# Turning key pages on VectorE in 32x32 blocks, with query rows and score rows laid out for it, in a hybrid decoder step

## The reference, cut to what matters

```python
h = rmsnorm(x, norm_g)
proj = jnp.einsum('bsd,de->bse', h, w_in)                  # 544 x 1024 by 1024 x 5632
q, k, v, g_a, u, v_s, g_b, m_a, m_b = jnp.split(proj, SPLIT_POINTS, axis=-1)
u = jax.nn.gelu(u)
v_s = layernorm(jax.nn.gelu(v_s), ln_g, ln_b)
...
# sample attention (moba_sample), for each of 8 samples, 16 cached pages of 128 keys x 8 heads x 64
k_full = cache_k[layer, page_table[:, :n_full * ppb]]
k_mean = jnp.mean(k_full.reshape(db, n_full, 256, N_HEADS, HEAD_DIM), axis=2)
gate = jnp.einsum('bthd,bnhd->bhtn', q, k_mean)            # 8 blocks of 256 keys
_, sel = lax.top_k(gate, 3)                                # three of them count
s_sel = jnp.einsum('bthd,bhtkd->bhtk', qf, k_sel) + bias
p = jax.nn.softmax(jnp.concatenate([s_sel, s_loc], axis=-1), axis=-1)
out = einsum(p_sel, v_sel) + einsum(p_loc, v_loc)          # per head and new row
...
y_a = attn * jax.nn.silu(g_a);  y_b = sgu * jax.nn.silu(g_b)
mixed = sigmoid(m_a) * (y_a @ w_pa) + sigmoid(m_b) * (y_b @ w_pb)
x = x + mixed @ w_o;  y = rmsnorm(x, final_norm_g)
```

## Time and profile before

| | |
|---|---|
| median of 3 runs | 582.92 us (582.87 to 583.2) |
| the profiled execution | 582.58 us |
| its span in the trace | 580.8 us |
| mean granted TensorE clock | 0.996 of full speed |
| busy: TensorE, VectorE, ScalarE, GpSimd | 98%, 54%, 36%, 4% of the span |
| the loop in the trace | 98.6 to 491 us |
| DMA over the span | 111.89 MB, mean 193 GB/s |

### The profile page before, as it was taken

One profiled execution on the slowest core, in us unless ns is written; L12 is line 12 of the kernel. 1 busy time (PEld: TensorE's weight loads), 2 busy tenths in 40 slices (PEclk: granted clock), 3 DMA queues, 4 the chain that ended last, 5 costly groups with the idle time before them and its releaser, 6 DMA issues.

```text
span 580.8 us, 14930 instructions
## 1 busy us (share of the span) xinstructions
PE 568.4 (98%) x6072; PEld 524.6 (90%) x6072; DVE 311.8 (54%) x733; ACT 210.4 (36%) x457; POOL 24.3 (4%) x39
## 2 busy tenths in 40 slices
PE   8999999999999999999999999999999999999994
PEld 6999999999999999999989998999999999998763
DVE  6622324344556465575757666785463354695514
ACT  5523222234333434444445442241252241234313
POOL 2101111000000000000000000010000000000002
PEclk9999999999999999999999999999999999999998
DMA  8447334765675756768577587875879856252003
GB/s 262 136 165 237 112 112 130 205 197 160 189 261 175 252 187 199 234 203 252 149 235 221 182 269 250 276 247 170 258 243 331 279 185 252 67 186 82 2 8 145
DMA packets 73421, 111.89 MB, mean 193 GB/s; under 512 B 5485, under 2 KB 35194, under 8 KB 73354
## 3 DMA queue, kind: packets, MB, share of 16 engines
q1 hardware_dynamic: 71978, 107.33, 57.7%
q0 software_dynamic: 1232, 3.36, 2.0%
q10 hardware_dynamic: 144, 0.26, 0.1%
HBM read 106.39 MB, written 4.53 MB: 191 GB/s over the span
## 4 chain that ended last, share of the span: by engine, by line
PE 93%; DVE 3%; ACT 1%; issue 1%; POOL 0%; POOLq 0%; DVEq 0%; ACTq 0%
PE BK L520 42%; PE BK L666 9%; PE BK L540 8%; PE BK L872 7%; PE BK L678 6%; PE BK L692 5%; PE BK L602 2%; PE BK L743 2%; PE BK L750 2%; PE BK L554 2%; PE BK L761 1%; PE BK L797 1%; PE BK L892 1%; PE BK L587 1%; PE BK L575 1%
## 5 line engine op out<-in xcount | busy, mean ns | idle before, releaser
L520 PE MATMUL BK<-XH,WH 128*128 128x272 f32 x672 | 212.2, 316 | 0.0
L520 PE MATMUL BK<-XH,WL 128*128 128x272 f32 x672 | 194.6, 290 | 0.0
L520 PE MATMUL BK<-XL,WH 128*128 128x272 f32 x672 | 193.5, 288 | 0.0
L520 PEld LDWEIGHTS BK<-XH,WH 128*128 128x128 f32 x672 | 127.0, 189 | 8.7 <-issue 8.0
L520 PEld LDWEIGHTS BK<-XL,WH 128*128 128x128 f32 x672 | 127.4, 190 | 0.0
L520 PEld LDWEIGHTS BK<-XH,WL 128*128 128x128 f32 x672 | 126.7, 188 | 0.0
L1165 DVE TENSOR_TENSOR WL<-WRAW,WH 128x1024 fp32r<-128x1024 f32 x51 | 62.2, 1220 | 37.9 <-ACT WH L921 37.6
L666 PE MATMUL BK<-CST,KRAW 128*128 128x128 f32 x512 | 77.2, 273 | 1.4 <-DVE ATS L1354 0.9
L666 PEld LDWEIGHTS BK<-CST,KRAW 128*128 128x128 f32 x512 | 60.5, 141 | 3.2 <-issue 3.1
L1263 DVE COPY KT<-BK 128x512 f32<-128x512 f32 x64 | 44.0, 687 | 35.3 <-PE BK L666 35.2
L921 ACT ACTIVATE WH<-WRAW 128x1024 fp32r<-128x1024 f32 x52 | 54.9, 1056 | 18.6 <-PE BK L540 18.6
(11 more groups left out here) (205 smaller groups left out, 796.6 us busy)
## 6 DMA issues: line engine op xcount, KB each, us to landing
KRAW<-in_cache_k SPq DMA_DIRECT2D x128, 256.0 KB, 3.5
VRAW<-in_cache_v SPq DMA_DIRECT2D x120, 256.0 KB, 3.9
WRAW<-in_w_in SPq DMA_DIRECT2D x21, 1024.0 KB, 5.5
WO<-in_w_o SPq DMA_DIRECT2D x4, 1024.0 KB, 7.9
XR<-in_x_prompt SPq DMA_DIRECT2D x4, 512.0 KB, 5.2
VEX<-in_cache_v SPq DMA_DIRECT2D x8, 256.0 KB, 5.1
WRAW<-in_w_pb SPq DMA_DIRECT2D x4, 512.0 KB, 6.3
WRAW<-in_w_pa SPq DMA_DIRECT2D x4, 512.0 KB, 5.8
```

The source lines that it names most:

```text
L520: last = mm(BK[h][:, 0:HALF], w[:, n % 2, k, :], x[:, k, cols], start=(i == 0 and w is WH and x is XA), stop=(i == KC - 1 and w is WL))
```

## The change

**Keys.** `turn_page` and both `page_out` are gone. VectorE turns each page with one operation, `dve.transpose`, from KRAW to KT. It turns every 32x32 block of the 128x512 page in its place: what was key 32g + m in partition, column 32f + d, stands afterwards in partition 32g + d, column 32f + m. The partitions so keep the key's quarter g, and only the lower five bits are swapped. `KR` goes from 5 to 4, the places of KT from 6 to 8.

**Scores.** A matmul sums over partitions, and these now mix four key quarters with 32 values of the head's width. So the queries are spread: QW holds, for each of 16 slices f of the width and each quarter, the 4 new rows of one sample at 8 columns of its own and zeros elsewhere. `page_scores` then sums over k (two halves of the head's width for two heads, each in its own columns) for each head pair c, with a moving operand that takes 32 columns from each of four pages. The rows of a score bank are now (head pair, key quarter, head of the pair, new row), its columns (page, key in the quarter). Sixteen matmuls before the loop and a copy bring the query rows (QR); GpSimd spreads those of one sample into QW (`query_rows`, four operations each). SCB is doubled (BK4 and BK2).

**Statistics.** All sums and masks follow the new rows: 128 rows of local scores, constant matrices OVER and TOTAL in place of SUM, 40 columns of R. `choose` writes the masked scores as a copy of all 512 columns (SC), and ScalarE takes one exponential over it. The local probabilities are turned by VectorE. The values' rows VS stand in all four partition groups.

**Values.** A page is now loaded as keys (a t) by b, 32 partitions of four rows each, four pages side by side: `load_v` works by fours, in six places (VRAW, parts of G and QK that are free by then, VEX).

**Moved.** GpSimd takes `split_lo` of tiles 14 to 45, the gate product and YBL. Blocks of prompt attention start at t % 16 in (5, 10, 15) from step 5. The steps of a sample's chain are now 16b + 18 (gate sums), 20 (exponentials), 22 (turn of the probabilities), 24 (sums), 37 and 44 (output), and `LAG` is 24. The constants of the layer norm load at step 72 instead of 83, `YBH` is written at 117 instead of 111.

```diff
-KR = 5
+KR = 4
-KB = 6
+KB = 8
...
-LAG = 20
+LAG = 24
...
+                    page = sp.snap(v_regs[j], min_val=0, max_val=cache_v.shape[1] - 1)
+                    sp.dma_start(VP[place][32 * j:32 * j + 32], cache_v[0, bass.ds(page, 1)].rearrange("a (b t) h d -> (a t) b (h d)", b=4)
+                                 ).then_inc(v_ld[place], 16)
...
-                for c in range(PAIRS):
-                    last = pe.transpose(BK[2 + i % 2][:, c * P:(c + 1) * P], KRAW[:, i % KR, c * P:(c + 1) * P], IDN)
-                last.then_inc(kt_pe, 1)
...
-                pe.wait_ge(kt_act, 2 * q + 2)
-                pe.wait_ge(kt_dve, 2 * q + 2)
+                pe.wait_ge(kt_ok, 4 * q + 4)
...
-                    for j in range(4):
-                        last = mm(SCB[32 * j:32 * j + 32, x * P:(x + 1) * P], QC[:, b, c, :], KT[:, (4 * q + j) % KB, c, :],
-                                  start=(c == 0), stop=(c == PAIRS - 1))
+                at4 = 4 * (q % 2)
+                for k in range(4):
+                    for c in range(PAIRS):
+                        f = 4 * c + k
+                        last = mm(SCB[b % 2][32 * c:32 * c + 32, x * P:(x + 1) * P], QW[:, f, :], KT[:, at4:at4 + 4, 32 * f:32 * f + 32],
+                                  start=(k == 0), stop=(k == 3))
...
+            def page_turn(i):
+                dve.wait_ge(k_ld[i % KR], 16 * (i // KR + 1))
+                wait(dve, sc_pe, (i - KB) // 4 + 1)
+                dve.transpose(KT[:, i % KB, :], KRAW[:, i % KR, :]).then_inc(kt_ok, 1)
...
-                dve.tensor_scalar(EB[:], OWS[:], NEGM[:], None, ALU.add).then_inc(eb_ok, 1)
+                wait(dve, pt_pe, b)
+                dve.tensor_tensor(SC[:].rearrange("p (n k) -> p n k", n=8), SCB[b % 2][:].rearrange("p (n k) -> p n k", n=8),
+                                  bass.AP(sel.tensor, sel.offset, [list(sel.ap[0]), [1, 8], [0, 64]]), ALU.add).then_inc(eb_ok, 1)
...
+            def split_lo(n):
+                pool.wait_ge(w_hi, n + 1)
+                if n == N_QKV + 2:
+                    pool.wait_ge(w_lo, n)
+                pool.tensor_tensor(WL[:, n % 2], WRAW[:, n // 2 % 2, :, n % 2 * P:(n % 2 + 1) * P], f32(WH[:, n % 2]), ALU.subtract).then_inc(w_lo, 1)
...
+            def query_rows(b):
+                wait(pool, sc_pe, 4 * b)
+                own = CST[:, C_OWN:C_OWN + 4]
+                for x in range(4):
+                    q, w = QR[:, x, TD * b:TD * b + TD], QW[:, x, 4 * (x // 2):4 * (x // 2) + TD]
```

More of the change, by code:

```diff
@@ L157, in values_step, with value_place, load_step, gate_step @@
     return CLOSE.get(q, 4 * q + LAG)
+def value_place(q):
+    same = [p for p in range(q) if PLACE[p] == PLACE[q]]
+    return PLACE[q], len(same) + 1, same[-1] if same else None
+def load_step(q):
+    first = {1: 8, 11: 64, 25: 113, 26: 115, 27: 117}
+    return first[q] if q in first else values_step(value_place(q)[2])
+def gate_step(b):
+    return 16 * b + 18 if b < NB - 1 else 129
+def exp_step(b):
+    return 16 * b + 20 if b < NB - 1 else 130
+def probs_step(b):
+    return 16 * b + 22 if b < NB - 1 else 132
+def sum_step(b):
+    return 16 * b + 24 if b < NB - 1 else 135
+def scale_step(b):
+    return 16 * b + 37 if b < NB - 2 else 131 if b < NB - 1 else 138
+def out_step_of(b):
+    return 16 * b + 44 if b < NB - 2 else 132 if b < NB - 1 else 139
+def sample_at(t, step):
+    for b in range(NB):
+        if step(b) == t:
+            return b
+    return None
 LAST = [4, 0, 1, 2, 3]
@@ L446, in _ @@
                 if m == 4:
[L447 to L448 removed]
+                    load_v(0)
             for t in range(STEPS):
@@ L587, in rows @@
                     pe.transpose(bp[:, r * P:(r + 1) * P], src[:, r * P:(r + 1) * P], IDN)
-                pe.transpose(bs[0:NSR, 0:P], src[:, SEQ:ROWS], IDN).then_inc(rows_pe, 1)
+                if n < 8:
+                    pe.transpose(bs[0:NSR, 0:P], src[:, SEQ:ROWS], IDN).then_inc(rows_pe, 1)
+                else:
+                    pe.transpose(bs[0:NSR, 0:P], src[:, SEQ:ROWS], IDN)
+                    for g in range(1, 4):
+                        last = mm(bs[32 * g:32 * g + 32, 0:P], src[:, SEQ:ROWS], IDN, start=True, stop=True)
+                    last.then_inc(rows_pe, 1)
             def early(n, h):
@@ L633, in _ @@
                     rows(n - 1)
+                if n == 5:
+                    for x in range(4):
+                        for b in range(4):
+                            last = mm(BK[2][32 * b:32 * b + 32, x * P:(x + 1) * P], IDN[:, 32 * x:32 * x + 32], QT[:, :, SEQ:ROWS], start=True, stop=True)
+                    last.then_inc(qr_pe, 1)
                 if n == 9:
@@ L680, in page_scores @@
[L680 to L693 removed]
+                    pe.wait_ge(qw_ok, b + 1)
@@ new lines, in page_scores, with page_values @@
+                    wait(pe, pt_ok, b - 1)
+                at4 = 4 * (q % 2)
[4 more added lines that the diff above has]
+                                  start=(k == 0), stop=(k == 3))
+                last.then_inc(sc_pe, 1)
+            def page_values(q):
+                b, x = q // 4, q % 4
+                place, loads, _ = value_place(q)
+                pe.wait_ge(v_ld[place], 64 * loads)
+                if x == 0:
+                    wait(pe, ots_ok, b)
+                    pe.wait_ge(pt_ok, b + 1)
+                for p in range(4):
+                    for c in range(PAIRS):
+                        last = mm(OUT[32 * c:32 * c + 32, 0:P], PT[:, x, 32 * p:32 * p + 32], VP[place][:, p, c * P:(c + 1) * P],
+                                  start=(x == 0 and p == 0), stop=False)
@@ L1058, in prompt_out @@
                 wait(act, av_pe, i)
-                copy(APT[:, 0, 0:n], BK[6][:, 0:n]).then_inc(a0_ok, 1)
+                for e in range(2):
+                    copy(APT[:, e, 0:n], BK[6 + e][:, 0:n]).then_inc(a0_ok, 1)
             def mix_high(m):
```

495 lines of the change are left out of this document (230 added, 265 removed).

## The result

The changed kernel takes 564.9 us (median of 4 runs, 563.75 to 568.94) against 582.9 before: a ratio of 0.9704, 95% interval 0.9655 to 0.9752. It is faster, by 18 us, where 45 were forecast, and it lies above the stated range (526 to 560). The profiled execution took 564.61 us, its span 562.8. In the numbers of all kernels an execution over 1.5% above the fastest of the same kernel is left out, since it belongs to a slower state of the chip (one of e5, two of e10).

The account below looks back on a forecast made before the run. TensorE's instruction stream was taken as the bound: 526.2 us, plus 3 for choices, 3 for steps 91 to 102, 3 for late loads and 0.5 for the loop's start, gave 535.7 of span, forecast 537.5 us. Range: 526 to 560.

Parts of the forecast that it names:

- the start: Start of the loop: 0.5 us added to the span.
- TensorE's stream: TensorE's own instructions over the span: 580.8 us before, 526.2 after; loop about 345 us, some 9 of them idle.
- The four-run operand: Score matmuls reading 32 columns from each of four pages: no added cost; at half rate, 564 us, chance 0.04.
- The turn: VectorE's turn of a whole key page: 0.69 us each, 88 us for 128 pages.
- Splits on GpSimd: 32 weight splits moved to GpSimd: 2.38 us each, 76 us in all, hidden with 4 us to spare.
- The choices: VectorE's choice of blocks delays a page turn: TensorE waits 1.2 us for samples 4 and 5, 0.6 for 6.
- Steps 91 to 102: Layer norm, last gates and choice leave VectorE almost no slack: 3 us of waiting, 0 to 6.
- Late loads: Same bytes in less time, four key buffers instead of five: 3 us of waiting, between 0 and 10.
- The rival: Value loads to 32 partitions, 1.3 to 1.7 times as slow, become the bound: 557 us, chance 0.15.
- the load case: Value loads become the bound: 541 to 567 us, taken as 557, chance 0.15; the range included half of it.
- VectorE in the middle: VectorE bounds steps 54 to 110, by turns of 1.2 us or standing during GpSimd's splits: 552 us, chance 0.13.
- Slower than before: VectorE's page turns fill the old loop from 2.0 us each; at 2.2 us, 613 us, chance 0.05.

Follow-up runs that it names:

- e5: e1 with the mask added in place in the bank and ScalarE's exponential reordering the score columns: 538.29 us.
- e10: The changed kernel with only the bursts of loads (layer norm constants, extra value groups) spread over more steps: 564.76 and 570.62 us.
- e2: The changed kernel with each value page loaded to all 128 partitions, rows misplaced: 535.94 us.
- e3: The changed kernel with value pages loaded only once per place, 104 of 128 value loads left out: 532.54 us.
- e4: The kernel before with the changed kernel's value loads alone, each starting after its whole group of four was used: 593.78 us against 582.9.
- e1: The changed kernel with each value page on every fourth partition of the whole range, the masked copy reordering columns to match: 543.45 us.
- e7: The changed kernel with each value page on every second partition of one half of the range, rows misplaced: 568.23 us.
- e8: e2 with the 32 weight splits moved back from GpSimd to VectorE: 538.47 us.
- e12: e2 with each key page turned twice on VectorE, one turn behind the other: 565.06 us.
- e6: e5 with VectorE turning the next step's page ahead of the choice of blocks instead of behind it: 538.34 us.
- e11: e2 with three places for key pages instead of four: 547.92 us.

## Why the prediction was wrong

**The sum was right except for one term, the loads.** e2 has the changed kernel's whole program but for where the values land, and takes 535.9 where 537.5 were summed. (The terms as written add up to 537.8: 535.7 of span, 1.8 and 0.3. The lower end of the range, 526, leaves out 0.5 of the start and these 2.1.) Term by term, in e2 or in the changed kernel:

- TensorE's stream: the loop was to be 345 us, with 9 of them idle; e2 has 345.4, with 7.75 idle.
- The four-run operand: 276 ns mean in e2, as L678 before. Nothing, as taken.
- The turn: 0.69 us taken, 0.70 measured. Splits on GpSimd: 2.38 taken, 2.40 measured, and none was waited for.
- The choices: 3 us taken (1.2, 1.2 and 0.6); the waits at the scores of steps 84, 100 and 116 are 1.4, 1.1 and 0.5 us in e2, 3.0 together, with the forecast's order of operations.
- Steps 91 to 102: 3 us taken; no wait stands there in e2 besides the one for step 100. In part that was made up by 1.7 us of waits around steps 66 and 82 (for R and APX), which no term had. So it is partly luck that the total came out so close.
- Late loads: 3 us taken; 3.4 by e2 less e3, in e2, where the waits at steps 80 and 128 (1.5 and 1.4 us) stand behind turns that waited for a key page. But in the changed kernel itself the shape of the values' loads adds 29 us to that: its loop is 374.4 us against e2's 345.4, TensorE idle 30.8 us against 7.75.

**The step that failed** is this term, late loads, "3 us, between 0 and 10", and with it the paragraph that put the values' loads aside as a rival with a chance of 0.15. The term was worked out from the rate of the old shape ("full would be 331" GB/s), as if four pages on 32 partitions each held the queues no longer than four on 128. Measured are some 251 GB/s with the queues full, and 32 us in place of the 3: the 3.4 of e2 and the 29 of the shape.

The rival had the mechanism, named the sign for it (0.84 of the queues' time late in the loop) and gave it 557, or 567 by the page's ratio; measured are 564.9. Its factor of 1.3 to 1.7 holds too. In the loop the queues were busy 0.92 x 374.4 = 344 us against 0.78 x 345.4 = 269 in e2, 75 more. The values' 16,384 packets, at the 99 ns that a 2 KB packet takes on average in e2's loop, are 101 us of the 16 queues. So the new shape makes at most 176 of 101, a factor of 1.7 (estimated, since some of the 75 are other loads'). In e4, where the queues have room, it is 0.81 x 401.4 less 0.71 x 392.4, 46 us more on some 106 (104 ns a packet), a factor of 1.4.

What was wrong was the weight. The nearest row (64 partitions of BSB in 4.1 us) excluded nothing, as the text says itself. The only measured numbers on this shape were those of the Trainium skill, "SBUF — State Buffer", section on door 1: 32 partitions reach half of the ports, 189 GB/s against 328. They spoke against the forecast, and the forecast stayed with the side for which there was no number at all. By the page's rule 1.7 was to be expected, and the trace agrees where the queues are full. The page's formula also gives the ports of e1 and e7: bits 2 to 4 and bit 6 of the partition's number name the port. Every fourth partition takes in all of them, every second of one half only half; the times, 543 and 568 us, agree. That it is ports and not something else that the reach of the range decides is the page's account; the runs show the reach alone.

The range ended at 560 because it took in "half of the load case". With the whole of that case it would have gone to 567 and held the time.

**VectorE in the middle** (0.13) is half confirmed. The exclusion with GpSimd exists: some operations of 0.72 us took up to 2.5. The Trainium skill, "SBUF — State Buffer", who interferes with whom, states it for instructions of VectorE with two SBUF inputs, and the trace agrees: turns, which have one, never took over 0.72 us. The prediction said that in the trace before the two engines never meet in such a pair. That was a misreading: near the end they do, and there it was GpSimd that stood. Its operation took 0.55 us by itself and 0.99 when it was issued 0.2 us into one of VectorE's with two SBUF inputs:

```profile
570.64 0.55 POOL L1655 TENSOR_TENSOR RSTD<-MS,NHALF 128x1 f32<-128x1 f32 x1 [7.04 <-DVE MS L1581]
...
574.47 0.99 POOL L1655 TENSOR_TENSOR RSTD<-MS,NHALF 128x1 f32<-128x1 f32 x1 [0.93 <-DVE MS L1581]
```

```profile
574.31 0.74 DVE L1588 SCALAR_TENSOR_TENSOR FX<-FX,RSTD,FG 128x512 f32<-128x512 f32 x1
```

But the exclusion cost VectorE only some 5.5 us in e2 (2 of 8 operations of L1352, one of L1477, one of L1371), and e8, where no split can meet them, is not faster. e12 shows where that engine would become the bound: at 1.4 us a turn 29 us are lost, where the rival had 15 at 1.2.

**Slower than before** needed turns above 2 us; e12's pair of 1.4 gives 565. **The clock.** While TensorE waits often, its granted clock falls at times, which the forecast had left out. In the changed kernel TensorE stood for 1.9 us before 358.8; from 360.4 on the row is:

```profile
360.40:363.40 3.00, 3.00 (x16) 3.00 (x15) 2.72 (x12) 0.22 (x1) 0.00 (x0) 0.50 1.07 227
```

The clock there is 0.50, the lower of its two levels (1.2 GHz). In the whole loop TensorE was busy 343.6 us for what takes it 337.7 in e2. So of the 29 lost us 23 are waits, and 6 are longer busy time, which the lower clock accounts for. The clock was as low from 305.6 to 312 us, in and behind the longest wait. e2, whose waits are short, has 1.00 over its loop.

**Left open**: why e5 and e6 stay some 2.5 to 5 us above e2 by their ratios (the two were measured on another chip than e2); how much of e4's 11 us comes from its later loads; and the share of the step from five places to four, of which e11 only shows the next step, from four to three, at 12 us.

## What to carry to other kernels

When a change alters the shape of a load, work out which destination partitions it reaches, and price the load by bytes and by reach, even where the change is about something else. Moving work off the bound engine shortens the time in which the same bytes must come, so a load that is now slower meets a demand that is now higher: the same shape cost 11 us in the old loop (e4) and 29 in the new one. Here 32 partitions in steps of four did what 32 in a row could not, with nothing but another order of columns ahead of it (e1, 8 us above e2).
